# Value products of a sliding-window attention: v_hi and v_lo side by side in one stationary block, halves added on VectorE

## The reference

```python
s = jnp.einsum('bnqkgd,bnskd->bnkgqs', q, k) * (HEAD_DIM ** -0.5)
...
pr = e / (jnp.sum(e, axis=-1, keepdims=True) + jnp.exp(sink - m))
return jnp.einsum('bnkgqs,bnskd->bnqkgd', pr, v)
...
yb = o.reshape(B, T, ATTN_WIDTH) * jax.nn.silu(za)
```

## Time and profile before

| | us |
|---|---|
| median of 3 runs | 1253.31 (1252.24 to 1255.3) |
| the profiled execution | 1254.71 |
| its span in the profile | 1252.9 |
| TensorE matmul busy | 1215.4 (97% of the span) |
| VectorE busy | 540.8 (43%) |
| ScalarE busy | 419.1 (33%) |
| GpSimd busy | 409.6 (33%) |

### The profile page before, as it was taken

The page is one execution under the profiler, slowest core; times in us unless marked ns, Lnnn a source line. Parts: engine busy times, 40 slices in busy tenths (PEclk is TensorE's granted clock), DMA queues, the critical chain, the costliest instruction groups (busy, mean ns, idle before and its releaser), DMA issues.

```text
span 1252.9 us, 19582 instructions
## 1 busy us (share of the span) xinstructions
PE 1215.4 (97%) x7688; PEld 1190.8 (95%) x7688; DVE 540.8 (43%) x906; ACT 419.1 (33%) x886; POOL 409.6 (33%) x189
## 2 busy tenths in 40 slices
PE   4899999899999999999999999999999999999997
PEld 4899889899999999999999999999999999999997
DVE  5869776211244444444433615481042151064321
ACT  4233333334267777777740101130020020041111
POOL 2333223223312222221144533424325335254410
PEclk8899999999999999999999999999999999999999
DMA  7313425531243434333351111116232233231211
GB/s 288 115 57 115 169 104 155 162 100 51 72 127 120 133 105 136 118 95 108 110 190 50 58 53 44 36 38 242 86 97 91 85 107 125 77 102 64 73 36 52
DMA packets 135948, 129.82 MB, mean 104 GB/s; under 512 B 40319, under 2 KB 123415, under 8 KB 135887
## 3 DMA queue, kind: packets, MB, share of 16 engines
q1 hardware_dynamic: 118487, 102.25, 26.6%
q10 hardware_dynamic: 17400, 26.71, 5.8%
HBM read 93.25 MB, written 37.71 MB: 105 GB/s over the span
## 4 chain that ended last, share of the span: by engine, by line
PE 88%; DVE 9%; DMA 1%; issue 1%; ACT 0%; SPq 0%; ACTq 0%; DVEq 0%
PE ps L576 75%; PE ps L770 4%; PE ps L748 2%; PE ps L758 2%; DVE sa L993 1%; DVE xn L938 1%; DVE sa L979 1%; DVE m_lo L942 1%; DVE sa L989 1%; DVE stack L973 1%; DVE hs L981 1%; DVE stack L971 1%; PE ps L631 1%; PE ps L603 1%; PE ps L687 1%
## 5 line engine op out<-in xcount | busy, mean ns | idle before, releaser
L576 PE MATMUL ps<-m_hi,w_hi 128*128 128x352 f32 x2016 | 664.5, 331 | 8.3 <-DVE m_lo L942 8.3
L576 PE MATMUL ps<-m_lo,w_hi 128*128 128x352 f32 x2016 | 650.0, 323 | 0.0
L576 PE MATMUL ps<-m_hi,w_lo 128*128 128x352 f32 x2016 | 435.9, 324 | 0.0
L576 PEld LDWEIGHTS ps<-m_hi,w_hi 128*128 128x128 f32 x2016 | 381.0, 189 | 12.6 <-issue 6.9
L576 PEld LDWEIGHTS ps<-m_lo,w_hi 128*128 128x128 f32 x2016 | 380.9, 189 | 1.0 <-issue 1.0
L576 PEld LDWEIGHTS ps<-m_hi,w_lo 128*128 128x128 f32 x2016 | 345.5, 189 | 0.0
L511 POOL TENSOR_TENSOR w_hi<-raw_a,w_one 128x1024 fp32r<-128x1024 f32 x42 | 80.9, 1926 | 778.4 <-PE ps L576 527.1
L513 POOL TENSOR_TENSOR w_lo<-raw_b,w_hi 128x1024 fp32r<-128x1024 f32 x42 | 111.4, 2652 | 3.3
L513 POOL TENSOR_TENSOR w_lo<-raw_a,w_hi 128x1024 fp32r<-128x1024 f32 x42 | 109.6, 2609 | 3.3
L511 POOL TENSOR_TENSOR w_hi<-raw_b,w_one 128x1024 fp32r<-128x1024 f32 x42 | 89.9, 2141 | 0.0
L1070 DVE TENSOR_TENSOR pt_lo<-ps,pt_hi 128x512 fp32r<-128x512 f32 x64 | 41.2, 686 | 58.5 <-ACT pt_hi L1402 58.5
(11 more groups left out here) (183 smaller groups left out, 1158.3 us busy)
## 6 DMA issues: line engine op xcount, KB each, us to landing
raw_a<-in_w_in SPq DMA_DIRECT2D x26, 512.0 KB, 3.7
raw_b<-in_w_in SPq DMA_DIRECT2D x26, 512.0 KB, 4.0
qk_d<-qkst ACTq DMA_DIRECT2D x10, 1056.0 KB, 4.3
gate_d<-gst ACTq DMA_DIRECT2D x16, 528.0 KB, 4.3
gin<-gate_d SPq DMA_DIRECT2D x16, 528.0 KB, 3.6
qt<-qk_d SPq DMA_DIRECT2D x32, 256.0 KB, 3.2
xT_d<-sa SPq DMA_DIRECT2D x4, 1056.0 KB, 7.4
yb_d<-sa SPq DMA_DIRECT2D x1, 4224.0 KB, 12.9
```

The source lines that it names most:

```text
L576: last = nc.tensor.matmul(ps[:, 3 * parity + c, 0:CH], w, x[:, k, CH * c:CH * c + CH], start=(k == 0 and w is wh and x is src_hi), stop=(k ...
```

## The change

`vt` keeps each of v_hi and v_lo once: a stationary block is now v_hi in columns 0 to 63 and v_lo in columns 64 to 127. For each key block it is multiplied with pt_hi and with pt_lo, so a unit has four matmuls of 512 columns instead of six (v_lo·pt_lo, which was left out, is now among them). The output has v_hi's part in partitions 0 to 63 and v_lo's part in 64 to 127. VectorE copies the upper half into a new SBUF tile `v_low`, adds it to the lower half in PSUM, and only then gates, now both even and odd heads from the lower half. Between these steps it waits for its own semaphore `low_step`. `att_read`, which frees the bank, is still counted by the last gate operation. `load_v` has one DMA instead of two. `vt` shrinks by 4 KB in each partition and `v_low` takes 2 KB.

```diff
-            vt = sb("vt", [P, 2, NKV, 2 * P], F32R, scope=s3)
+            vt = sb("vt", [P, 2, NKV, P], F32R, scope=s3)
+            v_low = sb("v_low", [HD, G * P], scope=s3)
...
-                for c in range(2):
-                    dst = vt[:, m // 4, m % 4, :].rearrange("p (s c e) -> p s c e", s=2, c=2)[:, :, c]
-                    sp.dma_start(dst.bitcast(F32), v_d[t, :, m % 4, :].rearrange("p (s e) -> p s e", s=2))\
-                        .then_inc(v_loaded[m % 4], 16)
+                sp.dma_start(vt[:, m // 4, m % 4, :].bitcast(F32), v_d[t, :, m % 4, :]).then_inc(v_loaded[m % 4], 16)
...
-                pe.wait_ge(v_loaded[kv], t * 32 + 32)
+                pe.wait_ge(v_loaded[kv], t * 16 + 16)
...
                 for s in range(2):
-                    for a, b in ((0, pt_hi), (0, pt_lo), (1, pt_hi)):
-                        last = nc.tensor.matmul(ps[:, bank, :], vt[:, s, kv, P * a:P * a + P], b[s][:],
-                                                start=(s == 0 and a == 0 and b is pt_hi),
-                                                stop=(s == 1 and a == 1))
+                    for b in (pt_hi, pt_lo):
+                        last = nc.tensor.matmul(ps[:, bank, :], vt[:, s, kv, :], b[s][:],
+                                                start=(s == 0 and b is pt_hi), stop=(s == 1 and b is pt_lo))
                 last.then_inc(att_done, 1)
...
                 dve.wait_ge(att_done, att_round("V", u) + 1)
+                o = ps[:, att_bank("V", m), :]
+                v.tensor_copy(v_low[:], o[HD:P]).then_inc(low_step, 1)
+                dve.wait_ge(low_step, u * 2 + 1)
+                v.tensor_tensor(o[0:HD], o[0:HD], v_low[:], ALU.add).then_inc(low_step, 1)
+                dve.wait_ge(low_step, u * 2 + 2)
                 for q in range(2):
-                    half = slice(64 * q, 64 * q + 64)
-                    o = ps[half, att_bank("V", m), :].rearrange("p (a q n) -> p q a n", q=2, n=P)[:, q]
-                    dst = sa[half, 2 * kv:2 * kv + 2, tok]
-                    last = v.tensor_tensor(dst, o, dst, ALU.mult)
+                    dst = sa[64 * q:64 * q + 64, 2 * kv:2 * kv + 2, tok]
+                    heads = o[0:HD].rearrange("p (a q n) -> p q a n", q=2, n=P)[:, q]
+                    last = v.tensor_tensor(dst, heads, dst, ALU.mult)
                 last.then_inc(att_read, 1)
```

More of the change, by code:

```diff
@@ L295, in build @@
             sem("key_copied"), sem("s_read"), sem("s_shift"), sem("s_exp"), sem("s_prob"), sem("spt_copied"))
-        att_done, att_read = sem("att_done"), sem("att_read")
+        att_done, att_read, low_step = sem("att_done"), sem("att_read"), sem("low_step")
         masks_loaded, zero_done = sem("masks_loaded"), sem("zero_done")
```

## The result

The changed kernel took 1264.35 us (median of 5 runs, 1263.39 to 1267.94) against 1253.31 (median of 5 runs on the same chip, 1251.17 to 1255.43): ratio 1.009, 95% interval 1.0077 to 1.0104. The forecast was 1266.5, slower. Its profiled execution took 1264.35, with a span of 1262.5, 9.6 more than the span before.

A forecast was written before the change was run, and what follows sets the result against it. TensorE, busy for 97% of the span, was taken to bound the kernel. -14.8 us of matmuls + 28.2 of stalls = +13.4 on 1254.7, giving 1268.1; as a median 1266.7, stated as 1266.5, range 1256 to 1275.

The forecast's parts named there:

- TensorE's gain: Two of six 512-column matmuls go in each of 32 units: 64 x 0.232 = 14.8 us less.
- VectorE's links: Copy and add before the bank is free, 0.69 us each plus 0.03 for each wait, 1.44 us together.
- A: Time that copy and add with their waits put before the bank's release: 1.44 us, from 1.17 to 1.70.
- the late start in the loop: First VectorE operation after V's end starts 0.14 us late in the loop, 0.04 in written-out units.
- rival 2: Within 0.3%: copy at twice the speed, start after V 0.04 us instead of 0.14 in the loop; 1256 us, chance 0.07.
- The stall: TensorE's next scores wait for the freed bank: 0.96 us in 24 loop units, 0.86 in 6 before, 28.2 us.
- What moved at nothing: Waits for T0, T1 and pt_lo, DMA, memset and ScalarE's work after the last unit: shifts said to cost no time.
- The first: Copy and add fit beside the scores and projection step before the bank is needed; the time falls to 1238.5, chance 0.09.
- the threshold of 0.99: Break-even length of copy and add with waits: 30 stalls of 0.49 us each equal the 14.8 us saved.
- The third: TensorE's granted clock falls after its stops, adding 51 us: about 1317, chance 0.04.
- The fourth: A removed matmul is worth less than its spacing: at 0.16 us each the gain is 10.2, time 1271; chance 0.02.

The follow-up runs named there:

- The links alone: Changed kernel with six matmuls for each unit again, copy and add kept: 1279.14 us against 1254.04 for the kernel before, ratio 1.0199.
- half links: Changed kernel with copy and add on 256 of the 512 columns: 1248.13 us against 1254.04 for the kernel before, ratio 0.9948.
- the gain alone: Changed kernel without copy and add, each gate operation reading its own half: 1240.04 us against 1254.04 for the kernel before, ratio 0.9881.

## Why the prediction was right

**TensorE's gain** was 14.8 us by the earlier trace rows; alone it was 14.9 by the ratio and 14.7 in the stretch. The Trainium skill's 131 ns (TensorE: Matmul & The Clock Gate, section Back-to-back issue gap) would have given 8.4; this kernel's matmuls of 512 columns start every 0.23 us, four of them in 0.93 (572.73 to 573.66).

**VectorE's links**, the copy and the add with their waits, A = 1.44, were priced from rows on 128 partitions. By line and form the changed kernel has

```profile
L1075 DVE COPY v_low<-ps 64x512 f32<-64x512 f32 x32 | 22.2, 693 | 33.1 <-PE ps L768 33.1
L1077 DVE TENSOR_TENSOR ps<-ps,v_low 64x512 f32<-64x512 f32 x32 | 22.1, 691 | 1.1
```

Neither half of the partitions nor PSUM as the output changed anything: 0.693 and 0.691 for a copy and an add. Starts are 0.73 apart. So A is 1.46, and the chain from V's end to the gate's end 2.45 where I had 2.44. Two errors cancelled in it: the late start in the loop went away from the first operation, as rival 2 had it, and came back ahead of the gate (575.28 to 575.42), whose address comes from a register in the loop. That these two were equal and opposite was luck; the prediction had not thought of the second.

**The stall** was the term that was mis-sized, by a tenth of a microsecond 30 times: forecast 28.2 us, measured 25. I had counted 0.96 in the loop and 0.86 before it. Measured by the first matmul of the next step: from V's end to it are 3.08 us (573.82 to 576.90) after, and 2.22 before (566.41 to 568.63), so 0.86; in a written-out unit 0.75. The row of the kernel before for that step, from the unit of the earlier trace rows:

```profile
568.63 0.32 PE L576 MATMUL ps<-m_hi,w_hi 128*128 128x352 f32 x1
```

I had put 0.08 for TensorE to see the semaphore, and it was 0.06; and I had added 0.03 for a restart, where a restart gives back 0.05: S1's weight load comes 0.91 later than before (2.51 instead of 1.60 after V's end), but the row of its first matmul begins with it instead of 0.16 after it. 24 x 0.86 + 6 x 0.75 = 25.1 us instead of 28.2. The links alone cost as much (25.1 in the medians, 22.3 to 27.6 by the interval of the ratio, 24.8 in the stretch), and with the gain it makes +10.3; measured were 11.0 in the median and 10.1 in the stretch. The forecast was +13.4.

**What moved at nothing** did so: no wait of TensorE for T0, T1 or pt_lo, even with a stall 0.73 longer. ScalarE's work after the last unit moved as far as said and stayed in front of its wait for TensorE: 0.40 us of that wait are left of 1.83, where the forecast moved it by 1.44.

**The rivals.** The first, that the links fit, was refused by the lengths of the operations. That the change would be a gain with short enough links was right: half links (A = 0.92) came out faster than before, by 5.9 us. But the threshold of 0.99 was too low; with the margins as they were measured (0.60 us in the loop, 0.71 before it) it is an estimated 1.1. The second needed a copy at twice the speed. The Trainium skill has up to 2x for a copy with a PSUM operand (VectorE: DVE Perf Modes, section The perf-mode tier table), but the prediction's 0.39 us overlooked that the same page, in section Why PSUM operands drop a tier, leaves fp32 at 1x; the trace agrees with that, 0.693 for 512 columns, no faster than the add. The third did not come: the clock stayed at 1.00 with stops nearly twice as long. The fourth was refused by the gain alone.

## What to carry to other kernels

An engine that is busy for 97% of the span gains from less work only if the release of its next buffer stays inside the margin that it had; take that margin from the timeline (here 0.6 us), and compare it with the price of what is put in the way, not the price with the idle share of the other engine. If work must be added behind a matmul, order it so that the buffer is free first: with nearly the same work, sum to SBUF, release, then gate, a loss of 0.9% became a gain of 1.0%. In a loop, an operation with its address in a register, or with a second wait on a register's value in front of it, started about 0.1 us late behind a semaphore here, so the first operation behind it had better be one without. And when a margin is read from one unit, look whether the next unit has the same one.

## What the runs showed of the hardware that I had not expected

- A TensorE that stops at a semaphore in front of a weight load loses less than the load is late: 0.91 us later at the load (2.51 after V's end instead of 1.60), 0.86 at the first matmul of the following step. With three lengths of stop the stretch grew by 8.8, 24.8 and 46.6 us, where the profile counts 9.4, 25.5 and 47.3 us of idle time ahead of the loads.
- The delay of about 0.1 us in loops sticks to the operation, not to the place: 0.14 ahead of the gate with `tok` in its address, 0.13 ahead of a copy that only had one more wait with a register in front of it. A single wait on a register's value is not enough: copy and add of the changed kernel have one each in the loop and start after 0.04. In the written-out units, where both are constants, the same copy with its two waits started after 0.04 (360.89 to 360.93) and the gate of the changed kernel too (369.28 to 369.32).
- A VectorE operation that writes PSUM costs what one that writes SBUF costs: 0.691 us for the add of 512 columns, against 0.686 for the subtraction of the earlier trace rows; 0.424 for the add of 256 columns in the kernel with half links, against 0.417 for that into `o_sum`.
